# Trainium2 kernel of two transformer blocks: the order of the expert loads in SyncE's DMA queue, from the second pair of experts on

## The chip, the cores and the metric

The program runs on one core of one Trainium2 chip. The metric is the device time of one execution in microseconds. The runs of the kernel before took 2704.24, 2704.27 and 2704.9 us, with a median of 2704.27 us.

## The reference

A sequence of 256 tokens with 1024 channels goes through two blocks, in float32. The first has two layers, each with four mixers (sparse attention, retention, an RWKV recurrence, a short convolution), a gated sum of their results, cross attention and an MLP. The second has one layer with a linear recurrence and an attention, followed by a gated MLP, and one layer with gated linear attention, followed by a mixture of experts. The change touches the loads of that mixture alone:

```python
def moe_swiglu(hn, router, w1, w3, w2):
    t = hn.reshape(-1, d)
    logits = (t @ router).astype(jnp.float32)
    top_vals, top_idx = lax.top_k(logits, TOP_K)               # TOP_K = 2 of N_EXPERTS = 8
    top_w = jax.nn.softmax(top_vals, axis=-1)
    gates = jnp.sum(top_w[..., None] * jax.nn.one_hot(top_idx, N_EXPERTS, dtype=jnp.float32), axis=1)
    for e in range(N_EXPERTS):
        h_e = jax.nn.silu(t @ w1[e]) * (t @ w3[e])             # w1, w3: 1024 x 3584
        out = out + gates[:, e:e + 1].astype(t.dtype) * (h_e @ w2[e])   # w2: 3584 x 1024
```

## The kernel before

The experts are ranked by how many tokens chose them. Rank p (0 to 3) and rank p + 4 form pair p: a bigger and a smaller expert. Each computes only for its own tokens (up to 128 slots for the biggest one, 96 for the bigger ones of the later pairs, 64 for the smaller ones). The 3584 hidden channels are taken in 14 steps of 256 (`UPS`), so that there are 4 x 14 = 56 rounds, g = 0 to 55, and pair 0 is g below 14.

A round works on one slab of w1 and w3 together for each expert (2048 KB, the "up slab") and one slab of w2 for each (1024 KB, the "down slab"). TensorE's order is written out in lines 2009 to 2030. From g = 14 on it is, for each g: up work of the bigger expert on up slab g (`up_c`, lines 1866 and 1869), transposes of the hidden rows of g - 1 (`turn_c`, lines 836 and 1934), up work of the smaller expert on up slab g (`up_b`, line 1879), gathers of tokens for the next pair in four of the 14 rounds (line 1955), then down work of g - 1, bigger expert (`down_c`, lines 1908 and 1910) and smaller expert (`down_b`, line 1946). The results of a pair stay in PSUM over its 14 rounds; in the third round of the next pair ACT's queue stores them to HBM (`store_rows`), and in the last pair GpSimd fetches rows back with four indirect DMAs (line 826).

All weights are loaded by SyncE (SP), which issues its DMAs one after another and waits, before each, until the buffer is free. `Ring.load` (lines 611 to 621) is that wait and the issue. The buffers of the expert stage (lines 632 and 633):

```python
up_rings = (Ring("up_a", [slabA[:, 0, :], slabA[:, 1, :]], "up_a"), Ring("up_b", [fbT[:, 0:2048], fbT[:, 2048:4096]], "up_b"))
down_rings = (Ring("down_a", [slabB[:, 0, :], slabB[:, 1, :]], "down_a"), Ring("down_b", [fbT[:, 4096:6144], fbT[:, 6144:8192]], "down_b"))
```

The bigger expert's up slab has two buffers of its full size. The smaller expert's up slab is loaded in two halves of 1024 KB (`up_slab_parts`, lines 746 to 750), and its ring has room for two halves, which is one slab: half h of round g can be issued when `up_b` has used half h of round g - 1. Both down slabs have two buffers. In the trace, loads into `slabA` are the bigger expert's up slabs, loads into `slabB` its down slabs, and loads into `fbT` the smaller expert's halves and down slabs. `up_slab(g, 0)` loads the bigger expert's up slab, `down_slab(g, 0)` and `down_slab(g, 1)` the two down slabs; all of them do nothing for g above 55.

Of the kernel before, what the change touches and what calls it, by code (L numbers as in the profile page):

```python
# [52 lines left out]
PAIRS = NEXP // 2  # L53
STEP = 256
UPS = FFE // STEP
# [208 lines left out]
def build(nc, a, out):  # L264
# [61 lines left out]
    with ctx:  # L326
# [336 lines left out]
        def _(sp):  # L663
# [71 lines left out]
            def id_of(g, side):  # L735

                r = g // UPS + PAIRS * side
                if r not in of:
                    of[r] = sp.value_load(expert[:, r:r + 1], min_val=0, max_val=NEXP - 1)
                return of[r]  # L740

            def up_slab(g, side):
                if g < PAIRS * UPS:
                    up_rings[side].load(sp, [(whole, a["od_exp_w13"][bass.ds(id_of(g, side), 1), g % UPS, :, :].rearrange("e p n -> p (e n)"))])

            def up_slab_parts(g):
                if g < PAIRS * UPS:
                    v = a["od_exp_w13"][bass.ds(id_of(g, 1), 1), g % UPS, :, :].rearrange("e p (h n) -> p (e h) n", h=2)
                    for h in range(2):
                        up_rings[1].load(sp, [(whole, v[:, h, :])])  # L750

            def down_slab(g, side):
                if g < PAIRS * UPS:
                    down_rings[side].load(sp, [(whole, a["od_exp_w2_2"][bass.ds(id_of(g, side), 1), g % UPS, :, :].rearrange("e p n -> p (e n)"))])
# [2 lines left out]
            up_slab(1, 0)  # L757
            down_slab(0, 0)
            down_slab(0, 1)
            for g in range(PAIRS * UPS):  # L760
                up_slab_parts(g + 1)
                up_slab(g + 2, 0)
                down_slab(g + 1, 0)
                down_slab(g + 1, 1)

            for t in (1, 0):
                sp.wait_ge(sem("result_rows"), due("sp", "result_rows"))
# [3068 lines left out]
```

How the kernel before makes its waits and increments, by code:

```python
            def load(self, sp, parts, end=None):  # L611
                n, b = self.loaded, self.loaded % len(self.bufs)
                self.loaded += 1
                self.ends.append(end or (self.used, 1))
                if n >= len(self.bufs):
                    name, by = self.ends[n - len(self.bufs)]
                    sp.wait_ge(sem(name), due("sp", name, by))
                full = f"{self.name}_full{b}"
                for dst, src in parts:
                    sp.dma_start(dst(self.bufs[b]), src).then_inc(sem(full), up(full, 16))
# [1 line left out]
            def take(self, pe, parts=1):  # L623
                b = self.taken % len(self.bufs)
                self.taken += 1
                full = f"{self.name}_full{b}"
                pe.wait_ge(sem(full), due("pe", full, 16 * parts))
                return self.bufs[b]
# [32 lines left out]
        @block.sync  # L662
# [64 lines left out]
            for i in range(6):  # L727
                ringA.load(sp, [cols(a["od_w_in_2"], ODD_SLABS, 512 * i)], groups((2, 3, 4, 4, 4, 2)[i]))
                if i == 1:
                    ringB.load(sp, [cols(a["od_w_in_2"], ODD_SLABS, ODD_SLABS[0][0])], ("few_taken", 1))
            linear(a["od_w_out_2"][0], D, sums)
            sp.wait_ge(sem("experts_ranked"), due("sp", "experts_ranked"))
            of = {}
# [30 lines left out]
            for t in (1, 0):
                sp.wait_ge(sem("result_rows"), due("sp", "result_rows"))
                sp.dma_start(out[0, t * P:(t + 1) * P, :], x[:, t, :]).then_inc(sem("result_out"), up("result_out", 16))
```

## Time and profile before

| | |
|---|---|
| median of 3 runs | 2704.27 us |
| profiled execution, its own time | 2704.16 us |
| its span | 2702.4 us |
| TensorE busy | 2647.8 us, 98% |
| VectorE busy | 1331.8 us, 49% |
| ScalarE busy | 425.9 us, 16% |
| read from HBM | 614.70 MB |
| expert loads of SP | 168 of 1024 KB into fbT, 56 of 2048 KB into slabA, 56 of 1024 KB into slabB |

The span runs from the first to the last instruction. Busy time of TensorE counts matmuls whose ends are modelled. A weight load of TensorE (PEld) is an instruction of its own, and a wait before it holds the matmul too. The granted clock is 1.00 in all of the expert stage, the engine's full 2.4 GHz.

### The profile page before, as it was taken

To read this page: it belongs to the slowest core of one execution; us is meant where nothing else is said; L and a number is where in the kernel's file an instruction comes from. 1 tells how busy PE (TensorE), PEld (TensorE's weight loads), DVE (VectorE), ACT (ScalarE), POOL (GpSimd) and SP (SyncE) were. 2 spreads that over 40 slices of the span, in tenths; PEclk is the share of its full clock that TensorE was granted. 3 is DMA by queue.
4 is the path that set the end of the run, shared out by engine and by line. 5 is a ranking of instruction groups with operands and counts; after the bars stand their busy time and mean duration, and the time that the engine had idled before them with its cause. 6 is when DMAs were issued, how large, how long until landed. Compare 5 with 4: busy or idle time off the path is not lost.

```text
span 2702.4 us, 47623 instructions
## 1 busy us (share of the span) xinstructions
PE 2647.8 (98%) x20746; PEld 2031.1 (75%) x20746; DVE 1331.8 (49%) x2386; ACT 425.9 (16%) x854; POOL 109.2 (4%) x134
## 2 busy tenths in 40 slices
PE   9999999999999999999999999999999999999997
PEld 6789997776688989777686887856777666666664
DVE  3654675776365467577654665546772111111112
ACT  2220222101222122200133111320110000000000
POOL 0011400000001130000000000000000000000000
PEclk9999999999999999999999999999999999999999
DMA  6322443544233143344433443339999999999996
GB/s 274 119 108 78 180 142 117 195 172 164 104 146 121 58 189 133 140 161 183 164 125 133 164 187 126 125 124 423 422 395 414 422 417 417 423 419 417 421 422 249
DMA packets 66999, 620.99 MB, mean 230 GB/s; under 512 B 7584, under 2 KB 7968, under 8 KB 11488
## 3 DMA queue, kind: packets, MB, share of 16 engines
q1 hardware_dynamic: 63072, 602.26, 55.8%
q0 software_dynamic: 2720, 13.52, 1.3%
q8 instruction: 165, 2.70, 0.4%
q10 hardware_dynamic: 992, 2.10, 0.2%
q14 instruction: 50, 0.41, 0.0%
HBM read 614.70 MB, written 3.15 MB: 229 GB/s over the span
## 4 chain that ended last, share of the span: by engine, by line
PE 85%; DMA 7%; DVE 6%; ACT 1%; issue 1%; SPq 0%; DVEq 0%; ACTq 0%
PE ps L1445 11%; PE ps L857 9%; PE ps L1457 8%; PE ps L1879 7%; PE ps L1277 6%; PE ps L899 5%; PE ps L1869 4%; DMA fbT<-in_od_exp_w 4%; PE ps L1946 3%; PE ps L1839 2%; PE ps L1866 2%; PE ps L1908 2%; PE ps L836 2%; PE ps L1341 2%; PE ps L1289 2%; PE ps L1255 2%
## 5 line engine op out<-in xcount | busy, mean ns | idle before, releaser
L1869 PE MATMUL ps<-slabA,work 128*32 128x128 f32 x2016 | 228.0, 273 | 0.0
L1866 PE MATMUL ps<-slabA,work 128*32 128x384 f32 x2016 | 225.2, 488 | 0.0
L1879 PE MATMUL ps<-fbT,work 128*64 128x256 f32 x1792 | 209.0, 383 | 9.1 <-DMA fbT<-in_od_exp_w 9.1
L1869 PEld LDWEIGHTS ps<-slabA,work 128*32 128x32 f32 x2016 | 216.7, 110 | 0.0
L3633 DVE COPY work<-ps 128x192 f32<-128x192 f32 x42 | 15.0, 358 | 400.0 <-PE ps L836 400.0
L1277 PE MATMUL ps<-hT,slabA 128*128 128x256 f32 x832 | 188.9, 380 | 1.1 <-ACT work L2214 1.1
L1879 PEld LDWEIGHTS ps<-fbT,work 128*64 128x64 f32 x1792 | 122.0, 137 | 79.1 <-DMA fbT<-in_od_exp_w 18.1
L1277 PEld LDWEIGHTS ps<-hT,slabA 128*128 128x128 f32 x832 | 155.7, 190 | 23.4 <-ACT work L2214 1.9
L857 PE MATMUL ps<-hT,slabA 128*128 128x256 f32 x736 | 163.4, 381 | 0.0
L1445 PEld LDWEIGHTS ps<-work 128*128 128x128 f32 x1152 | 139.5, 192 | 21.5 <-issue 21.0
L857 PEld LDWEIGHTS ps<-hT,slabA 128*128 128x128 f32 x736 | 138.3, 190 | 20.5 <-issue 2.5
L2559 DVE TENSOR_TENSOR work<-work 128x256 f32<-128x256 f32 (+2 forms) x207 | 85.3, 412 | 129.3 <-ACT work L2186 100.0
L1445 PE MATMUL ps<-work 128*128 128x128 f32 x1152 | 143.9, 275 | 0.1
L1457 PE MATMUL ps<-work 128*128 128x512 f32 x296 | 138.9, 593 | 0.0
L2186 ACT ACTIVATE work<-ps 128x512 f32<-128x512 f32 x96 | 52.3, 545 | 459.1 <-PE ps L1445 459.1
L1908 PE MATMUL ps<-slabB,work 128*32 128x512 f32 (+1 forms) x1008 | 116.8, 489 | 0.9 <-DVE work L3634 0.9
L1910 PE MATMUL ps<-slabB,work 128*32 128x256 f32 x504 | 116.6, 381 | 0.0
L1445 PEld LDWEIGHTS ps<-hT,slabA 128*128 128x128 f32 x768 | 92.4, 192 | 23.7 <-issue 23.7
L1457 PE MATMUL ps<-slabB,work 128*128 128x512 f32 x222 | 108.2, 596 | 0.5 <-DVE work L2767 0.5
L1946 PE MATMUL ps<-fbT,work 128*64 128x512 f32 x448 | 107.8, 602 | 0.0
L1866 PEld LDWEIGHTS ps<-slabA,work 128*32 128x32 f32 x2016 | 78.9, 110 | 34.1 <-issue 33.3
L1445 PE MATMUL ps<-hT,slabA 128*128 128x128 f32 x768 | 94.2, 276 | 0.0
(555 smaller groups left out, 4256.5 us busy)
## 6 DMA issues: line engine op xcount, KB each, us to landing
fbT<-in_od_exp_w SPq DMA_DIRECT2D x168, 1024.0 KB, 11.9
slabA<-in_od_exp_w SPq DMA_DIRECT2D x56, 2048.0 KB, 15.7
slabB<-in_od_exp_w SPq DMA_DIRECT2D x56, 1024.0 KB, 15.8
slabA<-in_w_in SPq DMA_DIRECT2D x24, 2048.0 KB, 8.3
slabA<-in_mlp_w SPq DMA_DIRECT2D x16, 2048.0 KB, 9.4
slabB<-in_mlp_w SPq DMA_DIRECT2D x32, 1024.0 KB, 4.8
slabA<-in_ev_ffn_w SPq DMA_DIRECT2D x11, 2048.0 KB, 8.1
slabA<-in_xa_wkv SPq DMA_DIRECT2D x6, 2048.0 KB, 8.1
```

The lines of the kernel that those rows point to most:

```text
L857: last = mm(ps[0:rows, g % PROJ, c0:c0 + n], lhs(k), rhs(k), start=(k == 0), stop=(k == KD - 1))
L899: last = mm(ps[:, g, c * P:(c + 1) * P], one[:, k, :], two[:, k, :], start=(k == 0), stop=(k == 3))
L1277: last = mm(ps[:, b, 0:T], side["gates"][:, k, c % 4 * P:(c % 4 + 1) * P], hT[:, k, :], start=(k == 0), stop=(k == KD - 1))
L1445: last = mm(ps[:, bank, c * P:(c + 1) * P], lhs[:, k, :], rhs[:, k, :], start=(k == 0), stop=(k == 3))
L1457: last = mm(ps[:, b, :], lhs, rhs, start=(i == 0), stop=(i == steps - 3), skip_group_check=True)
L1866: mm(rows[QUAD * i:QUAD * (i + 1)], tokens, wk[:, :, 0:2 * MID], start=(k == 0), stop=(k == KD - 1), skip_group_check=True)
L1869: last = mm(rows[MID:P, :, 64 * i:64 * (i + 1)], tokens, wk[:, :, 2 * MID:T], start=(k == 0 and i == 0), stop=(k == KD - 1), skip_group_ch ...
L1879: last = mm(ps[SMALL * j:SMALL * (j + 1), 1, 0:2 * P].rearrange("p (w n) -> p w n", w=2), xs[:, KD // 2 * h + k, :], v[:, k, :, j * P:(j + ...
L1908: mm(sums_c[QUAD * i:QUAD * (i + 1), c0:c1], hidden_c(g)[:, j, QUAD * i:QUAD * (i + 1)], w2[:, j, c0:c1], **flags)
L1910: last = mm(sums_c[MID:P, T * i:T * (i + 1)], hidden_c(g)[:, j, QUAD * i:QUAD * (i + 1)], w2[:, j, 768:D], start=(first and j == 0 and i ! ...
L1946: last = mm(ps[SMALL * half:SMALL * (half + 1), 6, :], he[:, j, :], w2[:, j, half * 512:(half + 1) * 512], start=(g % UPS == 0 and j == 0) ...
L2559: V(v.tensor_tensor(o, i0, i1, ALU.add))
```

## The change

The loop that issues the expert loads is written differently. For pair 0 the order stays: up slab of the bigger expert of round g, down slabs of round g - 1, up slab of the smaller expert of round g. From round 14 on the smaller expert's up slab of round g is issued before the two down slabs of round g - 1.

```diff
             up_slab(1, 0)
             down_slab(0, 0)
             down_slab(0, 1)
-            for g in range(PAIRS * UPS):
-                up_slab_parts(g + 1)
-                up_slab(g + 2, 0)
-                down_slab(g + 1, 0)
-                down_slab(g + 1, 1)
+            up_slab_parts(1)
+            for g in range(2, PAIRS * UPS + 1):
+                up_slab(g, 0)
+                if g < UPS:
+                    down_slab(g - 1, 0)
+                    down_slab(g - 1, 1)
+                    up_slab_parts(g)
+                else:
+                    up_slab_parts(g)
+                    down_slab(g - 1, 0)
+                    down_slab(g - 1, 1)
```

## Rows read from the trace of the kernel before

**Rows 1.** The page: GB/s of the DMA engines in 40 slices; ACT's DMA queue.
```profile
GB/s 274 119 108 78 180 142 117 195 172 164 104 146 121 58 189 133 140 161 183 164 125 133 164 187 126 125 124 423 422 395 414 422 417 417 423 419 417 421 422 249
...
q10 hardware_dynamic: 992, 2.10, 0.2%
```

**Rows 2.** Busy time by stretch: PE, PEld, DVE, ACT, POOL, clock, DMA share, GB/s.
```profile
1950.00:2050.00 100.00, 100.00 (x1184) 75.33 (x1182) 68.20 (x128) 10.73 (x25) 0.00 (x0) 1.00 1.00 402
2060.00:2200.00 140.00, 138.97 (x1682) 95.89 (x1680) 17.48 (x59) 5.50 (x18) 0.00 (x0) 1.00 1.01 420
2200.00:2440.00 240.00, 239.62 (x2908) 166.51 (x2907) 28.22 (x82) 9.65 (x32) 0.00 (x0) 1.00 1.01 419
2500.00:2650.00 150.00, 144.24 (x1752) 96.89 (x1752) 18.90 (x51) 5.77 (x19) 3.83 (x4) 1.00 1.01 421
```

**Rows 3.** Waits of weight loads, 2057 to 2500, then 2500 to 2690: total, times, longest.
```profile
PEld ps L1879 <- DMA fbT<-in_od_exp_w: 4.0, 7, 1.0
...
PEld ps L1879 <- DMA fbT<-in_od_exp_w: 12.8, 16, 2.0
```

**Rows 4.** Timeline of one round (g = 27 to 29): start us, us, engine, line.
```profile
2243.30 3.67 PE L1879 MATMUL ps<-fbT,work 128*64 128x256 f32 x32
...
2245.43 2.05 SPq L621 DMA_DIRECT2D fbT<-in_od_exp_w  x2
...
2246.90 0.63 PE L1908 MATMUL ps<-slabB,work 128*32 128x512 f32 x3
...
2249.65 1.94 PE L1946 MATMUL ps<-fbT,work 128*64 128x512 f32 x8
...
2251.52 0.52 PE L1866 MATMUL ps<-slabA,work 128*32 128x384 f32 x3
...
2257.93 3.67 PE L1879 MATMUL ps<-fbT,work 128*64 128x256 f32 x32
...
2266.15 0.12 PEld L1866 LDWEIGHTS ps<-slabA,work 128*32 128x32 f32 x3 [0.81 <-issue]
```

**Rows 5.** Timeline of SP: issues of the slabA loads for g = 17, 28, 36, 42.
```profile
2064.74 0.33 SPq L621 DMA_DIRECT2D slabA<-in_od_exp_w  x1
...
2233.93 0.35 SPq L621 DMA_DIRECT2D slabA<-in_od_exp_w  x1
...
2350.90 0.33 SPq L621 DMA_DIRECT2D slabA<-in_od_exp_w  x1
...
2445.61 0.34 SPq L621 DMA_DIRECT2D slabA<-in_od_exp_w  x1
```

**Rows 6.** Time to landing: slabA at 1813.84, g = 17, 28, 36, 42; fbT at 2047.7.
```profile
slabA<-in_od_exp_w SPq DMA_DIRECT2D x1, 2048.0 KB, 8.8
...
slabA<-in_od_exp_w SPq DMA_DIRECT2D x1, 2048.0 KB, 15.0
...
slabA<-in_od_exp_w SPq DMA_DIRECT2D x1, 2048.0 KB, 12.4
...
slabA<-in_od_exp_w SPq DMA_DIRECT2D x1, 2048.0 KB, 17.0
...
slabA<-in_od_exp_w SPq DMA_DIRECT2D x1, 2048.0 KB, 12.7
...
fbT<-in_od_exp_w SPq DMA_DIRECT2D x1, 1024.0 KB, 6.2
```

**Rows 7.** Timeline of PE: first use of slabA, g = 17, 36, 42; last half.
```profile
2083.22 0.52 PE L1866 MATMUL ps<-slabA,work 128*32 128x384 f32 x3
...
2369.54 0.52 PE L1866 MATMUL ps<-slabA,work 128*32 128x384 f32 x3
...
2463.50 0.52 PE L1866 MATMUL ps<-slabA,work 128*32 128x384 f32 x3
...
2672.13 1.95 PE L1879 MATMUL ps<-fbT,work 128*64 128x256 f32 x16 [1.51 <-DMA fbT<-in_od_exp_w]
```

**Rows 8.** The chain of waits: the gathers of one round.
```profile
2379.81 1.50 PE ps L1955 x8
```

## The prediction

> **What bounds the kernel now.** I read the page first: the row of GB/s by slices stands near 420 from slice 28 on, where it was mostly 60 to 190 before [rows 1]. That last third is the expert stage, 56 rounds g of 6.29 MB each. Below, U(g) is the bigger expert's up slab (2.10 MB), H0(g) and H1(g) are the halves of the smaller expert's up slab (1.05 MB each), D(g) and d(g) the two down slabs (1.05 MB each). Second view, busy time by stretch: TensorE is busy without a gap and yet the DMA engines move 419 to 421 GB/s; only from 2500 on does TensorE lack 5.8 us in 150, and in 1950 to 2050, where its rounds are longer, the rate falls to 402 [rows 2]. So two limits lie almost on each other. 6.29 MB at 421 GB/s are 14.9 us. The timeline gives TensorE's own round: the smaller expert's up work starts at 2243.30 and again at 2257.93, 14.63 us, with the down slabs from 2246.90 to 2251.5 and the bigger expert's up work from 2251.52 [rows 4]. Where both run freely TensorE is 0.3 us a round the faster, so every stock of landed slabs melts; the rounds with four gathers of the next pair's tokens in them (four each in pairs 0, 1 and 2, 1.50 us longer [rows 8]) fill it up again. Third view, who waited for whom: weight loads waited 4.0 us for H halves between 2057 and 2500 and 12.8 us from 2500 to the end, and for hardly anything else that comes by DMA [rows 3]. H is the slab with one buffer only: its half can be issued only when the half before it has been used, SP stands there, and all that is behind it stands too.
>
> The measure for all that follows is the stock s: how long U(g) lies landed before TensorE takes it. From issue, time to landing and first use [rows 5, 6, 7]: U(17) 2064.74 + 15.0 = 2079.7, used 2083.22, s = 3.5; U(28) 2233.93 + 12.4 = 2246.3, used 2251.52, s = 5.2; U(36) 2350.90 + 17.0 = 2367.9, used 2369.54, s = 1.6; U(42) 2445.61 + 12.7 = 2458.3, used 2463.50, s = 5.2. At U(36) TensorE was being held by H1, which lands last before its use. So before the change the stock that can be spent is s - 1.6.
>
> **What is removed and added.** Nothing: the same 280 expert loads of the same sizes, the same waits, the same arithmetic. Pair 0 (g below 14) keeps its order. No instruction of TensorE, VectorE or ScalarE moves. SP's burst in a round is the same five issues of 0.33 us each; nothing else hangs on SP there, and POOL's and ACT's own DMAs don't pass through its queue. I cost all this at nothing.
>
> **What is moved.** Order before: U(g), D(g-1), d(g-1), H0(g), H1(g). After: U(g), H0(g), H1(g), D(g-1), d(g-1). Two effects.
>
> First, which slab binds when bytes are short. Transfers land one behind another, 2.5 us per MB (14.9 / 6 by the rate). With U(g) landing at L: H0 at L+2.5, H1 at L+5.0, D(g-1) at L+7.5, d(g-1) at L+9.9. Uses, by the timeline's distances [rows 4]: H0 at L+6.4 (2257.93 - 2251.52), H1 at L+8.2, D at L+10.0 (2246.90 is 3.6 behind 2243.30), d at L+12.7 (2249.65). All have at least 2.6 us to spare, so U itself binds, at s = 0. Before, H1 bound at s = 1.6. The stock can now be used to the end: a gain of 1.6 us wherever it melts. At the very end, TensorE stood 1.51 us for the last H1 at 2672.13 [rows 7]; with that half landed 5 us earlier this wait goes: -1.5 us. What is late next there is D(55): it lands at L+12.4 and is not used before d(54)'s work ends, L+12.7 and 1.9; it is hidden.
>
> Second, how much stock the queue can build. Before, when SP is let go by H0's buffer, U(g+1), D and d (4.2 MB) are behind the H pair and mostly still to land. After, only U stands between, since D and d now queue behind H. From the moment H0(28) is issued, 2245.43, TensorE comes to U(29) at 2266.15: 20.7 us [rows 4]. After the change all of H0, H1, D, d, U stand behind that issue, 14.9 us of bytes plus the time that a load takes on top of its bytes. The first load of the stage, into an idle queue, took 8.8 us for 2.10 MB [rows 6], which is 5.0 of bytes and 3.8 on top. So U lands no earlier than 18.7 us after the issue, and s can't be above 2.0. Bounds for the 3.8, which no row shows for the new place: 0 below (cap 5.8, no stock seen is lost), and above it the cap falls to nothing at 5.8. I take 3.8; the 6.2 us of a 1.05 MB half with little ahead of it [rows 6], 3.7 over its bytes, is the nearest other row and agrees.
>
> The Trainium skill ("DMA: Bandwidth & Descriptors", section on the anatomy of one DMA on the SWDGE path) fits a load as about 2.0 us plus bytes over 436 GB/s, for GpSimd's queue. By that the five loads would take 2.0 + 14.4 = 16.4 us and the cap would be 4.3; our 8.8 us for 2.10 MB against its 6.8 speaks for the longer time, on SP's queue. With 4.3 the sum below would be -1.6 - 0.7 - 0.7 - 1.5 = -4.5 us, 2699.7.
>
> **The sum**, by spendable stock, in us of TensorE's waiting. Pair 1: before 3.5 - 1.6 = 1.9, after 2.0: 0. Pair 2: before 5.2 - 1.6 = 3.6, after 2.0: +1.6. Pair 3: the same, +1.6. Last H1: -1.5. At the seam (g = 14) D(13), d(13) and U(15) now wait until H1(13) is used; the DMA engines idle some 3 us there, which the larger stock of pair 0 pays and which is what the cap already says. Sum +1.7. The profiled execution took 2704.16 us (span 2702.4), within 0.1 of the median 2704.27: 2704.16 + 1.7 = 2705.9.
>
> **Rivals.**
> *The stock is not capped* (faster). If the load's extra time is hidden under the loads before it, s builds as before and is used to zero: -1.6 in each of three pairs, -1.5 at the end, -6.3: 2697.9. For it: in the melting stage U, H and D land evenly and the first issue may be untypical. Against: the rate falls to 402 as soon as TensorE's rounds are longer [rows 2], so the queue does run dry even with the old order's reserve. It can't be much better than this: at 421 GB/s the stage is nearly all bytes, and the 16.8 us of waits [rows 3] are mostly theirs.
> *The reserve is gone* (slower). In each of pairs 1 to 3 something else takes the DMA engines just when s stands at its cap: the stored rows, 2.10 MB in three parts [rows 1], are 1.7 us a time, in the third round of a pair, and s at U(17) stood low at 3.5. If nothing spendable is left there: +1.9 + 3.6 + 3.6 - 1.5 = +7.6, 2711.8. It decides if s is under 0.5 behind the cap, that is if the extra time of a load is over 5.3 instead of 3.8. Further on, two rounds need L + 8.4 to the next H0 issue and 18.7 to U, 27.1 against 29.8 of bytes; only with 2.7 us more of extra time would every round grow, so this loop is not at its limit.
> *Nothing shows*: bytes set both, the stocks differ but what is lost by the cap comes back by the 1.6: 2704.2, or 2702.7 with the last wait alone.
>
> **Numbers.** Forecast 0.45 (2703.5 to 2709); uncapped 0.20, half of it beyond 0.2% (the case of the middle cap lies within); reserve gone 0.20; nothing shows 0.15. A measurement of this kernel tells 0.2%, 5.4 us, from no change. Faster: half of the uncapped case and a little of forms that I don't see, 0.11. Slower: the reserve case less the part under 2709.7, and the upper edge of the forecast, 0.20. Same: 0.69. The range reaches into both side cases: 2698.5 to 2712.5; the forecast's own is 2703.5 to 2709.
>
> **What would show it.** Right: U(28) and U(42) land about 2 us before use instead of 5.2; waits of weight loads for the H halves from 2057 on near zero, and in their place waits of the bigger expert's up work for slabA, some 17 to 20 us in all; the last H half landed well before its use; GB/s in 2200 to 2440 a little under 419. The forecast is wrong if s at U(28) is still near 5 (faster), if waits for slabA appear in pair 1 from its third round on (slower), or if the down slabs become a wait, which the landing times above exclude with 2.6 us to spare.

## The result, and the profile after

| | before | after |
|---|---|---|
| median | 2703.9 us (10 runs, 2702.92 to 2706.62) | 2712.27 us (10 runs, 2710.34 to 2713.59) |
| profiled execution, its own time | 2704.16 us | 2711.36 us |
| its span | 2702.4 us | 2709.5 us |

The changed kernel is slower: ratio 1.0031, 95% interval 1.0023 to 1.0038, 8.4 us. The forecast was 2705.9 us and "the same". The time lies in the range and within 0.5 us of the rival called "the reserve is gone" (2711.8). All lines of code behind the loop have moved by 6: line 1866 is now 1872, 1879 is 1885, 1908 is 1914.

The page of the kernel after, GB/s by slices; it answers to [rows 1]:

```profile
GB/s 273 120 109 76 183 145 117 186 176 167 107 134 125 68 174 133 153 170 160 164 124 156 150 177 126 144 137 422 422 376 403 421 400 418 416 405 412 423 414 282
```

Busy time by stretch of the kernel after, with the columns of [rows 2] (PE, PEld, DVE, ACT, POOL, clock, DMA share, GB/s):

```profile
1950.00:2050.00 100.00, 100.00 (x1182) 75.39 (x1180) 68.02 (x126) 10.70 (x25) 0.00 (x0) 1.00 0.96 381
2060.00:2200.00 140.00, 136.89 (x1664) 94.89 (x1665) 17.45 (x59) 5.46 (x18) 0.00 (x0) 1.00 1.01 421
2200.00:2440.00 240.00, 236.22 (x2823) 163.83 (x2821) 28.16 (x82) 9.38 (x31) 0.00 (x0) 0.99 1.00 409
2440.00:2500.00 60.00, 60.00 (x744) 41.23 (x744) 8.08 (x21) 2.43 (x8) 0.00 (x0) 1.00 1.01 411
2500.00:2650.00 150.00, 142.03 (x1749) 99.33 (x1742) 19.17 (x51) 5.79 (x19) 3.83 (x4) 0.99 1.01 419
```

The DMA engines move less around the seam (381 in place of 402 GB/s), in 2200 to 2440 (409 in place of 419) and a little less in 2440 to 2500 (411 in place of 416). In the other two stretches the kernels differ by 1 and 2 GB/s. The bytes are the same, so the last expert slab must land later.

Who waited for whom, kernel after, 1830 to 2710 (total us, times, longest); it answers to [rows 3], and a weight load's wait holds some 0.8 us each of ordinary time:

```profile
PEld ps L1872 <- DMA slabA<-in_od_exp_w: 35.9, 24, 3.4
...
PE ps L1872 <- DMA slabA<-in_od_exp_w: 13.9, 12, 2.5
...
PEld ps L1885 <- DMA fbT<-in_od_exp_w: 0.9, 2, 0.6
```

In the kernel before, the same view has the matmuls waiting 9.1 us for halves H in fbT, and never for slabA. The wait has changed its slab, as predicted, and it has grown.

The timeline of SP after, around the seam; it shows the queue's two standstills:

```profile
2019.96 0.34 SPq L621 DMA_DIRECT2D slabA<-in_od_exp_w  x1
2030.55 2.05 SPq L621 DMA_DIRECT2D fbT<-in_od_exp_w  x2
2032.78 0.33 SPq L621 DMA_DIRECT2D slabB<-in_od_exp_w  x1
2033.30 0.33 SPq L621 DMA_DIRECT2D fbT<-in_od_exp_w  x1
2034.89 0.33 SPq L621 DMA_DIRECT2D slabA<-in_od_exp_w  x1
...
2047.36 2.06 SPq L621 DMA_DIRECT2D fbT<-in_od_exp_w  x2
2049.61 0.86 SPq L621 DMA_DIRECT2D slabB<-in_od_exp_w  x1
2050.64 0.57 SPq L621 DMA_DIRECT2D fbT<-in_od_exp_w  x1
2051.40 0.52 SPq L621 DMA_DIRECT2D slabA<-in_od_exp_w  x1
```

And the same of the kernel before, where two down slabs fall into the second pause (the last row, 9.79 us with two waits in it, is d(14) and the two halves of round 15):

```profile
2035.27 0.33 SPq L621 DMA_DIRECT2D slabA<-in_od_exp_w  x1
2038.29 0.33 SPq L621 DMA_DIRECT2D slabB<-in_od_exp_w  x1
2040.01 9.79 SPq L621 DMA_DIRECT2D fbT<-in_od_exp_w  x3
```

SP issues nothing from 2019.96 to 2030.55, with U(14) the last load in the queue, and again from 2034.89 to 2047.36, with D(13), d(13) and U(15) in it (4.2 MB, 9.9 us of bytes, against 12.5 us). At the end of both pauses the queue runs dry, and at the end of the first the more. The kernel after in 2028 to 2032 and 2046 to 2050:

```profile
2028.00:2032.00 4.00, 4.00 (x38) 2.68 (x39) 1.64 (x7) 0.60 (x1) 0.00 (x0) 1.00 0.36 123
2046.00:2050.00 4.00, 4.00 (x40) 2.65 (x38) 1.70 (x7) 0.28 (x1) 0.00 (x0) 1.00 0.74 242
```

The kernel before moves 414 and 393 GB/s there; the differences are 2.8 and 1.4 us at 422 GB/s. The kernel before in stretches of 20 us, 2000 to 2060:

```profile
2000.00:2020.00 20.00, 20.00 (x251) 15.60 (x249) 14.30 (x25) 2.06 (x5) 0.00 (x0) 1.00 0.98 373
2020.00:2040.00 20.00, 20.00 (x228) 13.96 (x228) 12.51 (x26) 2.69 (x6) 0.00 (x0) 1.00 1.01 412
2040.00:2060.00 20.00, 20.00 (x271) 15.72 (x263) 7.72 (x19) 0.94 (x3) 0.00 (x0) 1.00 1.00 412
```

The kernel after, the same stretches:

```profile
2000.00:2020.00 20.00, 20.00 (x249) 15.64 (x247) 13.91 (x25) 2.18 (x6) 0.00 (x0) 1.00 0.97 363
2020.00:2040.00 20.00, 20.00 (x229) 14.07 (x229) 11.11 (x23) 2.57 (x6) 0.00 (x0) 1.00 0.86 328
2040.00:2060.00 20.00, 20.00 (x268) 15.56 (x259) 9.11 (x21) 0.94 (x3) 0.00 (x0) 1.00 0.96 374
```

The differences, 10 + 84 + 38 = 132 GB/s for 20 us each, are 2.6 MB or 6.3 us at 422 GB/s; some 1.2 us of them are made up in the next 20 us (426 against 401).

Time to landing of U(16), U(28), U(42) after, issued at 2051.40, 2237.43 and 2453.69, and of the half H0(15) issued at 2047.36; it answers to [rows 6]:

```profile
slabA<-in_od_exp_w SPq DMA_DIRECT2D x1, 2048.0 KB, 15.9
...
slabA<-in_od_exp_w SPq DMA_DIRECT2D x1, 2048.0 KB, 15.4
...
slabA<-in_od_exp_w SPq DMA_DIRECT2D x1, 2048.0 KB, 15.1
...
fbT<-in_od_exp_w SPq DMA_DIRECT2D x1, 1024.0 KB, 7.5
```

First uses of slabA in the kernel after, g = 16, 17, 28, 36, 42, 55, and the first use of D(55); it answers to [rows 7]:

```profile
2068.21 0.52 PE L1872 MATMUL ps<-slabA,work 128*32 128x384 f32 x3
...
2083.91 0.52 PE L1872 MATMUL ps<-slabA,work 128*32 128x384 f32 x3 [1.00 <-DMA slabA<-in_od_exp_w]
...
2253.32 0.52 PE L1872 MATMUL ps<-slabA,work 128*32 128x384 f32 x3
...
2376.24 0.53 PE L1872 MATMUL ps<-slabA,work 128*32 128x384 f32 x3 [0.64 <-DMA slabA<-in_od_exp_w]
...
2470.03 0.52 PE L1872 MATMUL ps<-slabA,work 128*32 128x384 f32 x3
...
2671.21 0.52 PE L1872 MATMUL ps<-slabA,work 128*32 128x384 f32 x3
...
2687.88 0.63 PE L1914 MATMUL ps<-slabB,work 128*32 128x512 f32 x3 [0.94 <-DVE work L3640]
```

Landing is issue plus time to landing, and the stock s is first use less landing, for every round in the same way:

| g | U lands before | after | later by | s before | s after | TensorE later by |
|---|---|---|---|---|---|---|
| 14 | 2031.8 | 2031.4 | -0.4 | 8.0 | 7.9 | -0.4 |
| 15 | 2046.6 | 2050.4 | 3.8 | 7.4 | 3.2 | -0.4 |
| 16 | 2061.5 | 2067.2 | 5.7 | 7.0 | 1.0 | -0.4 |
| 17 | 2079.7 | 2083.9 | 4.2 | 3.5 | 0.0 | 0.7 |
| 22 | 2154.8 | 2159.5 | 4.7 | 1.6 | 0.0 | 3.1 |
| 25 | 2200.4 | 2204.2 | 3.8 | 5.8 | 3.7 | 1.8 |
| 28 | 2246.3 | 2252.9 | 6.6 | 5.2 | 0.4 | 1.8 |
| 36 | 2367.9 | 2376.2 | 8.3 | 1.6 | 0.0 | 6.7 |
| 39 | 2413.9 | 2420.5 | 6.6 | 4.2 | 4.2 | 6.5 |
| 42 | 2458.3 | 2468.8 | 10.5 | 5.2 | 1.3 | 6.5 |
| 55 | 2661.0 | 2671.2 | 10.2 | 1.3 | 0.0 | 8.9 |

The column "later by" is the main story. It grows in three places: at the seam (4 to 6 us), at the end of pair 1's gathers and just behind them (3.8 at g = 25, 6.6 at 28, 8.0 at 31) and at the end of pair 2's (7.9 at g = 40, 10.5 at 42; the 6.6 at g = 39 is low because the kernel before had U(39) late). At the ends of the gathers the kernel before was holding its highest stock. Elsewhere it moves by 1 to 2 us either way and gives nothing back for good: while bytes are short, time that the DMA engines stood idle doesn't come back. TensorE ends 8.9 us late at U(55), which is 10.2 less the stock of 1.3 that the kernel before still held there. Behind it 1.7 us come back: D(55) is first used at 2687.9, where it was 2680.7, 7.2 us later, and 7.2 is the difference of the two profiled executions.

### The profile page after: what moved, and what is told of

Its sections match the earlier page's. It is cut to its first block, busy times and chain, and to the rows that moved or that the text cites. A ratio compares the mean times of both kernels' runs of the same rounds, so it can differ in the third digit from the quotient of the medians.

```text
span 2709.5 us, 47623 instructions
## 1 busy us (share of the span) xinstructions
PE 2649.2 (98%) x20746; PEld 2036.6 (75%) x20746; DVE 1331.6 (49%) x2386; ACT 424.6 (16%) x854; POOL 109.1 (4%) x134
## 4 chain that ended last, share of the span: by engine, by line
PE 80%; DMA 11%; DVE 6%; ACT 1%; issue 1%; SPq 1%; DVEq 0%; ACTq 0%
PE ps L1451 10%; DMA slabA<-in_od_exp_w 9%; PE ps L863 9%; PE ps L1463 8%; PE ps L1283 6%; PE ps L1885 6%; PE ps L905 5%; PE ps L1875 4%; PE ps L1845 2%; PE ps L1872 2%; PE ps L842 2%; PE ps L1952 2%; PE ps L1347 2%; PE ps L1295 2%; PE ps L1261 2%; PE ps L1429 1%
## 5 line engine op out<-in xcount | busy, mean ns | idle before, releaser
L1872 PEld LDWEIGHTS ps<-slabA,work 128*32 128x32 f32 x2016 | 79.8, 111 | 50.5 <-DMA slabA<-in_od_exp_w 35.9
L1451 PEld LDWEIGHTS ps<-hT,slabA 128*128 128x128 f32 x768 | 92.4, 192 | 23.7 <-issue 23.7
## 6 DMA issues: line engine op xcount, KB each, us to landing
fbT<-in_od_exp_w SPq DMA_DIRECT2D x168, 1024.0 KB, 10.2
```

The costliest lines, as they stand in the source:

```text
L1451: last = mm(ps[:, bank, c * P:(c + 1) * P], lhs[:, k, :], rhs[:, k, :], start=(k == 0), stop=(k == 3))
L1872: mm(rows[QUAD * i:QUAD * (i + 1)], tokens, wk[:, :, 0:2 * MID], start=(k == 0), stop=(k == KD - 1), skip_group_check=True)
```

## The experiments

Every kernel was timed beside runs of the kernel before on the same chip; its median there was 2703.33 us (27 runs; e1 to e4), 2703.64 us (29 runs; e5 to e8) and 2703.64 us (27 runs; e9 to e11). The table is the overview; differences are from those medians.

| kernel | median us | ratio, 95% interval | difference |
|---|---|---|---|
| e1, one down slab behind the halves | 2704.53 | 1.0005 [0.9996, 1.0015] | +1.2 |
| e2, changed order from round 46 | 2701.96 | 0.9994 [0.9985, 1.0004] | -1.4 |
| e3, changed order, TensorE kept busy | 2712.36 | 1.0032 [1.002, 1.0045] | +9.0 |
| e4, changed order from 42 | 2705.09 | 1.0004 [0.9995, 1.0014] | +1.8 |
| e5, old order, four half buffers | 2705.26 | 1.0006 [0.9996, 1.0016] | +1.6 |
| e6, changed order, four half buffers | 2708.64 | 1.0019 [1.0009, 1.0028] | +5.0 |
| e7, changed order from 18 | 2709.13 | 1.0022 [1.0012, 1.0031] | +5.5 |
| e8, changed order in pair 1 alone | 2711.38 | 1.0029 [1.0019, 1.004] | +7.7 |
| e9, four half buffers, changed order from 18 | 2702.88 | 0.9996 [0.9987, 1.0005] | -0.8 |
| e10, changed order from 54 | 2702.74 | 0.9997 [0.9988, 1.0006] | -0.9 |
| e11, four half buffers, changed order from 54 | 2703.36 | 0.9998 [0.9989, 1.0007] | -0.3 |

**e1: which down slab stands behind the gate.** The gate is SP's wait, before each half, for that half's buffer. Against the changed kernel:

```diff
                 else:
+                    down_slab(g - 1, 0)
                     up_slab_parts(g)
-                    down_slab(g - 1, 0)
                     down_slab(g - 1, 1)
```

> Order from round 14 on: U(g), D(g-1), H0(g), H1(g), d(g-1): one down slab ahead of the halves, one behind. Theory of the capped stock: the smaller expert's halves have one slab of room, so SP stands at H0 until it is free, and all that stands behind H0 up to the next U must still land. Here that is 5.2 MB instead of 6.3, so U's stock can reach 2.0 + 2.5 = 4.5 us: U(28) lands about 3 to 4.5 us before use (0.4 in the changed kernel), the time comes out at 2702 to 2706, 6 to 10 us under the changed kernel. The rival, that the waits come from U being the slab that is short whenever H isn't last: U is still the last that binds (H1 lands 7.5 us behind U and is used 8.2 behind it, so both bind nearly together), and the time stays within 2 us of the changed kernel, 2710 to 2714.

Measured +1.2 us, U(17) with s = 1.5, U(28) 3.2, U(42) 3.0. U binds in the short rounds here too, at s = 0, and yet the kernel isn't slower than before by what can be told. So the binding of U by itself isn't what costs the 8 us. With one slab less behind the half, the DMA engines stand less:

```profile
1950.00:2050.00 100.00, 100.00 (x1182) 75.31 (x1180) 68.45 (x129) 10.50 (x25) 0.00 (x0) 1.00 0.99 393
...
2200.00:2440.00 240.00, 237.95 (x2893) 165.78 (x2893) 28.20 (x82) 9.41 (x31) 0.00 (x0) 1.00 1.01 417
```

393 lies in the middle between 402 and 381, 417 just under 419. The second MB behind the single buffer costs more than the first: the first brought +1.2 us, which is within its interval, the second 7.2.

**e2, e4, e7, e8, e10: where the order is changed.** The edit is the round from which it holds, here e7:

```diff
-                if g < UPS:
+                if g < 18:
                     down_slab(g - 1, 0)
```

with 46 (e2), 42 (e4) and 54 (e10) in its place, and in e8 `if g < UPS or g >= 2 * UPS`.

> The order of before up to round 45, the changed order from round 46 on, where the kernel before is short of bytes and holds no stock that a cap could take. Capped stock: nothing is lost, the 1.6 us between U's landing and its use and the 1.5 us of the last H1 are won, -3 us: 2701. Rival (the changed order itself costs TensorE waits for U in each round that is short of bytes): these ten rounds cost their part of the 8 us, some 2 to 4 us more than before, 2706 to 2708.

> The order of before for pairs 0, 1 and 2, the changed order for pair 3 (rounds 42 to 55) alone. Capped stock: U(42) has 5.2 us of stock when the order changes, and it falls to about 1 to 2 within two rounds, 3.2 us of the DMA engines' time are lost there, 3 us are won at the end: the time of before within 2 us (2702.5 to 2706). Rival (every short round costs): pair 3 costs its third of the 8 us, 2707 or more.

> The changed order from round 18 on instead of 14. The prediction compared the cap with the stock at U(17), behind the stored rows' bytes, and found nothing lost in pair 1; by the traces U(15) already lands 4.2 us later than before, at the seam. If the seam in front of the stored rows is what costs there, the change at round 18 gives most of it back: U(17) lands 4 us before use as with the old order, and the time is 2.5 to 4.5 us under the changed kernel, 2707.5 to 2710. Rival (the order costs in every round that is short of bytes): 4 rounds fewer of 42 give back under 1 us.

> The changed order in rounds 14 to 27 alone, the old one before and behind. Pair 1 then costs its 2 to 3 us as in the changed kernel, and pair 2 starts with a stock of 0.5 to 2 us where the old order has use only for what is over 1.6, so it lacks the 3.6 us that it had to spend: 4 to 7 us over before, 2707 to 2710. Pair 3 finds its stock rebuilt by pair 2's gathers and ends as before. Rival (the loss is spread evenly over the 42 rounds, 0.2 us each): a third of it, under 3 us over before.

> The changed order for the last two rounds alone (g from 54 on), otherwise the kernel before. Theory (all of the gain lies behind the last U): the last U lands within 1 us of before, D(55) is used 16.5 to 17 us behind it instead of 19.7, and the time is 2 to 3 us under before, 2700.5 to 2702. Rival (the switch itself idles the DMA engines by as much as it gives, since SP stands at H(54) with D, d and U(55) behind it): U(55) lands 2 to 3 us later and the time is that of before within 1 us.

Late starts (e2, e10) leave the landings nearly as they are (U(55) 1.1 us later in e2, 0.3 earlier in e10) and shorten what follows the last U. The first use of U(55) and of D(55) in e10:

```profile
2661.61 0.52 PE L1872 MATMUL ps<-slabA,work 128*32 128x384 f32 x3
...
2678.29 0.63 PE L1914 MATMUL ps<-slabB,work 128*32 128x512 f32 x3 [0.94 <-DVE work L3640]
```

U(55) is issued at 2644.2 and lands at 2660.7 in e10 (2661.0 before), and D(55) follows its landing by 17.6 us instead of 19.7, the use by 16.7 instead of 18.4. The gain of the medians, 0.9 and 1.4 us, is smaller than the 2.4 us of e10's profiled execution (2701.74 against 2704.16) and not clear of the interval; the expected 2700.5 to 2702 of e10 was missed by 0.7. e2's -1.4 is half of the 3 us expected, and its rival (2706 to 2708) is out.

Started at 42 (e4), with the stock of pair 3 at its height, the order takes s from 5.3 at U(42) to 1.2 at U(43), and the rate in 2440 to 2500 falls to 387 GB/s. The cap is real, and about 1. Started at 18 (e7) instead of 14, the kernel is 2.9 us less slow (5.5 against 8.4): that is the seam's share. e8, with the order in pair 1 alone, costs 7.7 us, more than the 4 to 7 expected and nearly all of the 8.4: the delay made in pair 1 stays to the end though the old order has come back and U(42) lies landed for 5.1 us again. That the cost were spread evenly over the three pairs is out. The costs of e7 and e8 don't add up to the 8.4, and the landings say why. The last U lands 7.8 us later than before in e7, 8.3 in e8 and 10.2 in the changed kernel. e7 and the changed kernel have the new order at their end, which gives 1.6 and 1.7 us back there; e8 hasn't.

**e3: the clock.** The granted clock of the changed kernel dips twice behind a long wait (last section). Five small matmuls into an unused bank were put at the start of seven rounds that wait:

```diff
+            FILLED = (17, 20, 31, 46, 48, 50, 52)
...
+                    if g in FILLED:
+                        for _ in range(5):
+                            mm(ps[:, 3, 0:P], ident, ident, start=True, stop=True, skip_group_check=True)
                     if g == 1:
```

> The changed kernel with five 128x128 matmuls into an unused PSUM bank put before the bigger expert's up work of rounds 17, 20, 31, 46, 48, 50 and 52, where TensorE then waits 1.1 to 2.5 us for U anyway; about 1.1 us of work. Theory that part of the loss is the clock: the two stretches of 3.4 us at a granted clock of 0.5 behind the waits of 2.4 and 2.5 us don't come, and up work there takes 6.4 us instead of 8.0: 3.3 us are won, 2709, no clock of 0.5 before the end. Rival (the clock's dips are paid back by slabs that land meanwhile): dips gone, time unchanged at 2712, or longer by what filler sticks out.

The dips were gone and the time the same, 2712.36 against 2712.27. Expected was 2709. The 1.6 us that a dip costs had come back already: the loads go on while TensorE is slow, and the two slabs behind the first dip lie landed for 1.5 and 1.2 us, in a stretch where all others have 0. In this stage, which waits for bytes, a slower TensorE was paid out of its own next waits.

**e5, e6: room for the halves.** Four buffers of a half from pair 1 on, so that a half's issue waits for a use two rounds back, and SP is hardly held by it. The branch for experts with more tokens than fit, which these inputs don't take, isn't served. The core of the edit:

```diff
+                self.bufs = [fbT[:, 0:2048], fbT[:, 2048:4096], prm[:, PARAM_AT["gw2"]:PARAM_AT["gw2"] + 2048], merged.rearrange("p k t -> p (k t)")]
+            def slot(self, n):
+                return n % 2 if n < 2 * UPS else n % 4
...
+                if n in (2 * UPS + 2, 2 * UPS + 3):
+                    sp.wait_ge(sem(("up_a", "down_a")[n % 2]), UPS)
+                elif n > 1:
+                    sp.wait_ge(sem("up_b"), n - 1 if n < 2 * UPS + 4 else n - 3)
...
-                        up_rings[1].load(sp, [(whole, v[:, h, :])])
+                        halves.load(sp, v[:, h, :])
```

e5 is this with the old order, e6 with the changed one.

> The order of before, and room for four halves of the smaller expert's up slab from pair 1 on instead of two: two more buffers lie where pair 0's sums of weights lay and are free from round 14 on. (The branch for experts with more tokens than fit, which these inputs don't take, isn't served by it.) Capped stock: SP no longer stands at the halves, the DMA engines can run ahead in rounds with gathers and pay for the later ones, and TensorE's 12 us of waiting behind round 14 shrink to under 4: 2692 to 2697. Rival (bytes alone set the stage's end, and the DMA engines already have no idle time): the time of before within 2 us.

> The changed order with the same room for four halves. If the loss comes from SP standing at the halves with the down slabs and the next up slab behind, the order no longer matters with this room: the same time as with the old order and the same room, within 2 us, so some 16 to 20 us under the changed kernel. Rival (the changed landing order costs by itself, or the late down slabs do): it stays 5 to 9 us over the old order with room.

e5 was to be 7 to 12 us faster and is 1.6 us slower than before, within the interval. Windows of e5:

```profile
1950.00:2050.00 100.00, 100.00 (x1184) 75.34 (x1182) 68.38 (x128) 10.60 (x25) 0.00 (x0) 1.00 1.00 405
2060.00:2200.00 140.00, 138.93 (x1682) 95.87 (x1682) 17.49 (x59) 5.75 (x19) 0.00 (x0) 1.00 1.01 422
2200.00:2440.00 240.00, 239.74 (x2909) 166.01 (x2905) 28.19 (x82) 9.41 (x31) 0.00 (x0) 1.00 1.01 422
...
2500.00:2650.00 150.00, 144.07 (x1740) 96.39 (x1742) 19.48 (x52) 5.75 (x19) 3.83 (x4) 1.00 1.01 422
```

Halves are issued some 7.5 us earlier and take 20 us instead of 12 to land (medians from round 18 on), so that they land some 0.9 us later than before; U(28) has 5.2 of stock, U(42) 5.1, U(36) 1.6, as before. 422 GB/s is the ceiling, and the kernel before stood at 420 and 419. There the halves had been short of bytes, not of room. e5 isn't free of a cost of its own: where the two new buffers come into use it moves 366 GB/s in 2040 to 2060 against 412 before, and its U(17) lands 1.1 us later. But from there to U(54) it stays later by 0.6 to 2.1 us, and the room wins nothing back. That 18 us of TensorE's waits were put down to a slab with one buffer said where the shortage shows, not what causes it.

e6 shows 422 from 2060 on as well, s = 3.3 at U(28) and 3.4 at U(42), and no idle time of the DMA engines behind the seam. So with room the order costs nothing to be seen there. But it is 3.4 us over e5, and its U(17) has s = 0. The extra buffers come only with pair 1: pair 0's two halves still gate the queue at the seam, with the new order behind them. In 2000 to 2060 e6 moves 360, 333 and 351 GB/s.

**e9, e11: room, and the seam left alone.** The edit of e5 with `g < 18` (e9) and `g < 54` (e11) as the start of the changed order.

> The changed order from round 18 on, behind the stored rows of pair 0, with room for four halves of the smaller expert's up slab (the branch for experts with more tokens than fit isn't served). Theory (a round is 14.8 us of bytes, the order costs only where SP stands at a half with D, d and U behind it, at the seam of round 14, and the order gives back 3 us at the end): no idle of the DMA engines from 2060 on, 421 to 423 GB/s, and 2702 to 2704 us, 2 to 3 us under the old order with room (2705.3) and 5 to 6 us under the changed order with room (2708.6). Rival (the order costs in each pair, room or not): 2707 to 2709 us.

> As the one before, with room for four halves (the branch for experts with more tokens than fit isn't served). Theory: the switch idles nothing, since the halves are issued long before; 3 us under the old order with room (2705.3), so 2702 to 2703. Rival (with room, what is behind the last U is already at its bytes and the order of the last slabs no longer counts): 2705 to 2706.

e9, its windows 2000 to 2060 and then 2060 to 2650:

```profile
2000.00:2020.00 20.00, 20.00 (x237) 15.15 (x235) 15.52 (x28) 2.06 (x5) 0.00 (x0) 1.00 0.99 382
2020.00:2040.00 20.00, 20.00 (x243) 14.95 (x241) 11.24 (x25) 2.69 (x6) 0.00 (x0) 1.00 1.00 401
2040.00:2060.00 20.00, 20.00 (x261) 15.10 (x261) 9.02 (x21) 0.61 (x2) 0.00 (x0) 1.00 0.90 363
...
2060.00:2200.00 140.00, 140.00 (x1703) 96.95 (x1691) 17.46 (x59) 5.79 (x19) 0.00 (x0) 1.00 1.01 422
2200.00:2440.00 240.00, 239.13 (x2907) 166.61 (x2905) 28.18 (x82) 9.52 (x32) 0.00 (x0) 1.00 1.01 422
...
2500.00:2650.00 150.00, 144.17 (x1745) 98.40 (x1745) 18.98 (x51) 5.74 (x19) 3.83 (x4) 0.99 1.01 422
```

2702.88 us, as expected (2702 to 2704), 5.8 us under e6. The difference of their windows 2000 to 2060, 22 + 68 + 12 = 102 GB/s for 20 us each, is 2.0 MB, 4.8 us. 38 of the 42 rounds that the change touches have its order here, and it costs nothing. What costs is that the loads behind a buffer still in use can't be issued while the queue runs dry. e11 (2703.36, 0.4 over its expected upper end) is the same as e9 within the intervals, and the profiled executions put what the order gives with room at the very end: from the first use of U(55) to the end of the span are 38.3 us in e9, 38.4 in e11 and 40.3 in e5. No version beats the kernel before by more than its interval; the fastest medians, e2's and e10's, are 1.4 and 0.9 us under it.

## Why the prediction was right, and where it was wrong

The measured time lies inside the stated range, by 0.2 us, and that is luck: the range reached so far only because it took in the side cases. The forecast's own range ended at 2709, the sum said +1.7 where the profiled executions differ by +7.2, and by the prediction's own yardstick of 5.4 us for "no change" the 8.4 us are the slower case that it gave 0.20. By its own steps, the terms of the sum against TensorE's delay in the table above (the stage itself starts 0.4 us earlier in the profile of after):

| term | predicted | measured |
|---|---|---|
| pair 1, U(14) to U(28) | 0 | +2.2 |
| pair 2, U(28) to U(42) | +1.6 | +4.7 |
| pair 3, U(42) to U(55) | +1.6 | +2.4 |
| last half | -1.5 | -1.7 |
| sum, with -0.4 for the start | +1.7 | +7.2 |

- **Both limits lie on each other** (right). e5 shows it best: 422 GB/s without a gap, and the time of before.
- **U binds, the other slabs have 2.6 us to spare** (right, to the tenth). In the short rounds of the changed kernel H0, H1, D and d lie landed for 4.0, 3.3, 2.6 and 2.9 us and U for 0.0. It isn't so in every round: in round 30, with the stored rows, and in round 51 D had 0.4 and 0.3 us left. Two weight loads waited 0.4 us each for a down slab, and no matmul did.
- **The last half** (right): -1.7 for -1.5, and e2 and e10 have it alone.
- **The cap** (right in kind, 1 us too high, and not for every round). From the issue of H0(15), 2047.36, to U(16) landed, 2051.40 + 15.9 = 2067.3, are 19.9 us, where I had 18.7; from H0(42) to U(43) they are 19.7. That leaves 20.7 - 19.8 = 0.9 of stock, and the table has 1.0 at U(16) and 1.3 at U(42); e4 has 1.2. So the time on top of the bytes was 5.0, not 3.8. Part of it is idle engines (242 GB/s in 2046 to 2050) although U(15) landed only at 2050.4, 3.0 us after H0(15) was issued: a load is told landed after its last bytes have moved. The first pause shows that alone: U(14) was the last load in the queue and landed at 2031.4, and in 2030 to 2031 the engines moved 16 GB/s. The second row for the 3.8, the half that took 6.2 us, was read wrongly: when it was issued at 2047.74, D(14) (2038.29 + 10.8 = 2049.1) and d(14) were still to land, and the engines moved 393 GB/s, so its 3.7 us were mostly other slabs' bytes. And "s can't be above 2.0" holds for rounds without gathers only: from H0(39)'s issue TensorE comes to U(40) after 23.7 us, U(40) lands after 19.6, and s is 4.2. The Trainium skill's fit ("DMA: Bandwidth & Descriptors", anatomy of one DMA on the SWDGE path) gives, as an estimate, 16.4 us for the five loads into an idle queue. From the issue of H0(14), with U(14)'s bytes moved, to U(15) landed were 19.8 us, which speaks against taking the fit over to SP's queue with several loads in it.
- **The step that failed: "Pair 1: before 3.5 - 1.6 = 1.9, after 2.0: 0".** I compared the cap with the stock at U(17). But U(17) lies behind the stored rows' round: before the change s had been 7.0 at U(16) and fell to 3.5 from there. The cap cuts at U(15) and U(16), from 7.4 and 7.0 to 3.2 and 1.0, and the fall of the next round comes on top. The true comparison is 7.0 - 1.6 = 5.4 spendable before against 1.0 after. The same in pairs 2 and 3: in the kernel before s fell from 6.9 at U(27) to 5.2 at U(28) and from 4.8 at U(30) to 3.1 at U(31), and again from 4.5 at U(44) to 1.6 at U(45), all of it behind the place where the cap cuts. With pair 1 put at 0 it measured +2.2, with pair 2 at +1.6 it measured +4.7. A cap must be set against the highest stock, and all drops behind it stay on the bill.
- **"At the seam the DMA engines idle some 3 us, which the larger stock of pair 0 pays"** (wrong). They idle some 2.8 us at the pause that it means and 5 with the pause of the next round, and no stock pays for idle DMA engines where bytes are the limit: it only puts off when the loss shows. e6 against e9 (4.8 us by the windows, 5.8 by the medians), e7 and e8 show it.
- **"Reserve gone"** named the outcome, its place (pair 1 from the third round on; the first wait is at U(17), in the fourth) and its size (+7.6), with a chance of 0.20. Its condition, s under 0.5 behind the cap, was met at U(17) (0.0) and U(28) (0.4), but in pair 3 only at U(45), and not by a time on top of 5.3: it was 5.0, and a cap of 1 with what came behind it was enough. How much of the fall from 7.0 to 3.5 at U(17) is the stored rows' own bytes wasn't tried.
- **Uncapped** is refuted by e4, **"nothing shows"** by the result.
- **The signs.** Weight loads waited 0.9 us for halves, near nothing as foretold, but 35.9 us for slabA where 17 to 20 were named; GB/s in 2200 to 2440 fell by 10 and not "a little"; U(28) and U(42) had 0.4 and 1.3 us of stock, not 2.

The forecast's unit was at fault too. Counting TensorE's stock pair by pair asks when the wait shows; counting the DMA engines' idle time asks what is lost. The second gives the result in one line: the last U 10.2 us later, less the stock of 1.3 us used up once, less 1.7 at the end, is +7.2.

## What to carry to other kernels

Where a queue of loads is at its ceiling of bytes, cost a new order by how long the queue stands at a gate with nothing ahead of it, at every place where the stock is being filled: that idle time came on the end here, less the little stock still held there. What is put behind a single-buffered load can't be issued before that buffer is free, so slabs with room to spare belong ahead of it; one slab moved behind it cost 1.2 us here (within its interval), two cost 8.4. And a wait for a slab in a single buffer isn't evidence that the buffer is the cause, as doubling it (e5) showed.

## What the runs showed of the hardware

**The clock behind a wait.** In the changed kernel TensorE waited 2.38 us until 2300.34 and went to its lower level, 1.2 GHz (a granted clock of 0.5), 1.3 us later; two-us stretches from 2300 on:

```profile
2300.00:2302.00 2.00, 1.66 (x29) 1.62 (x33) 0.00 (x0) 0.00 (x0) 0.00 (x0) 0.90 1.00 418
2302.00:2304.00 2.00, 2.00 (x23) 1.76 (x19) 0.00 (x0) 0.00 (x0) 0.00 (x0) 0.50 1.00 418
2304.00:2306.00 2.00, 2.00 (x34) 1.88 (x30) 0.00 (x0) 0.00 (x0) 0.00 (x0) 0.75 1.05 438
2306.00:2308.00 2.00, 2.00 (x36) 1.66 (x28) 0.00 (x0) 0.33 (x1) 0.00 (x0) 1.00 1.05 442
```

From the first use of U(31) to the smaller expert's up work were 8.1 us there instead of 6.4. Waits of 2.48 (the changed kernel again), 2.56 (e4) and 2.71 us (e9) came with the same fall, one of 2.32 us (e2) and one of 2.71 us (e6) were not; no wait of matmuls under 2 us in the expert stage was. So the length of a wait doesn't decide it alone.

**The ceiling.** A single core read 422 GB/s from HBM over some 600 us on end (e5, e9). The Trainium skill ("DMA: Bandwidth & Descriptors", where 436 GB/s comes from) says that for transfers between HBM and SBUF the limit of HBM for a core, some 358 GB/s, binds, a figure that it gets by halving a rate shared by two cores; the same section calls its own measured 425 GB/s near fabric-rate. The program here runs on one core, and its 422 are 18% above the first figure and agree with the second.

**The DMA share.** Beside 363 GB/s the share of busy DMA engines stands at 0.97 in one window (after) and at 0.90 in another (e9), beside 374 at 0.96, beside 328 at 0.86, and beside 422 at 1.01. It falls by less than the bytes do, and not evenly with them; a queue that runs dry for a part of a window is seen in the GB/s.
